# Column sums by transposes, two experts' gathers at a time, and 128-row spreading products in a three-network float32 kernel

## What is computed

```python
# first network, for each of 2 layers: nine modulation vectors of 1024 from c
mod = c_act @ ada_w[l] + ada_b[l]
sh1, sc1, g1, sh2, sc2, g2, sh3, sc3, g3 = jnp.split(mod, N_ADA, axis=-1)
...
x = x + 0.5 * g1[:, None] * swiglu(h, ff_w13[l, 0], ff_w2[l, 0])
# attention of the second and third network: norms over each head's 64 columns
q = rms_norm_2(q.reshape(B, S, FOX_HEADS, HEAD_DIM), fox_g_q[j])
k = rms_norm_2(k.reshape(B, S, FOX_HEADS, HEAD_DIM), fox_g_k[j])
...
# second network: top-2 of 8 experts, each 1024 -> 3584 (gate, up) -> 1024
top_logit, top_idx = lax.top_k(logits, TOP_K)
gates = jax.nn.softmax(top_logit, axis=-1)
ys = swiglu_2(tokens of expert e, w_gate[e], w_up[e], w_down[e]) * gate
out[token] += ys
```

## Time and profile before

| | us |
|---|---|
| median of 3 runs | 3297.51 |
| lowest and highest | 3294.65, 3300.77 |
| the profiled execution, its own time | 3293.94 |
| the profiled execution, span | 3292.1 |
| mean granted TensorE clock | 0.963 of full |

### The profile page before, as it was taken

The page is one execution under the profiler, slowest core; times in us unless marked ns, Lnnn a source line. Parts: engine busy times, 40 slices in busy tenths (PEclk is TensorE's granted clock), DMA queues, the critical chain, the costliest instruction groups (busy, mean ns, idle before and its releaser), DMA issues.

```text
span 3292.1 us, 49368 instructions
## 1 busy us (share of the span) xinstructions
PE 3153.1 (96%) x21206; PEld 2908.7 (88%) x21206; DVE 2261.7 (69%) x2574; ACT 1701.9 (52%) x1910; POOL 84.8 (3%) x163
## 2 busy tenths in 40 slices
PE   6999899999998999999989999999999999989999
PEld 6999899999988998899978888888888888889999
DVE  6686667677555555454575888888888888544575
ACT  4434343443534335443434777777777777444453
POOL 1010001011000000000000000000000000000000
PEclk9999899999988999999987999999999999989999
DMA  7685458678421653245412988989889889423353
GB/s 278 239 305 206 145 193 289 221 278 293 171 71 65 218 203 124 70 144 184 167 39 88 368 338 341 363 338 362 342 337 365 337 341 364 153 103 129 104 192 116
DMA packets 112319, 739.26 MB, mean 225 GB/s; under 512 B 12480, under 2 KB 12480, under 8 KB 32096
## 3 DMA queue, kind: packets, MB, share of 16 engines
q1 hardware_dynamic: 89424, 651.21, 53.1%
q0 software_dynamic: 22672, 84.84, 7.2%
HBM read 734.95 MB, written 1.05 MB: 224 GB/s over the span
## 4 chain that ended last, share of the span: by engine, by line
PE 79%; DVE 5%; ACT 2%; issue 1%; DMA 0%; DVEq 0%; ACTq 0%; POOLq 0%
PE ps L514 60%; PE ps L513 17%; PE ps L523 2%; DVE wlo L2702 2%; DVE AF L2684 1%; ACT whi L1823 1%; DVE att L2693 0%; DVE hl L2675 0%; DVE gf L2687 0%; ACT cv L1811 0%; DVE T L2675 0%; DVE AF L2675 0%; ACT hh L1811 0%; ACT L1811 0%; ACT AF L1811 0%
## 5 line engine op out<-in xcount | busy, mean ns | idle before, releaser
L2702 DVE TENSOR_TENSOR wlo<-ring,whi 128x2048 fp32r<-128x2048 f32 x620 | 1418.7, 2291 | 505.9 <-ACT whi L1823 505.5
L1823 ACT ACTIVATE whi<-ring 128x2048 fp32r<-128x2048 f32 x620 | 1186.0, 1915 | 342.9 <-issue 236.0
L514 PE MATMUL ps<-whi,AR 128*128 128x512 f32 (+1 forms) x2724 | 880.2, 398 | 0.4 <-DVE AF L2675 0.4
L514 PE MATMUL ps<-hh,whi 128*128 128x256 f32 x2464 | 707.5, 287 | 3.9 <-DVE wlo L2702 3.3
L514 PE MATMUL ps<-hl,whi 128*128 128x256 f32 x2464 | 701.3, 285 | 0.0
L514 PE MATMUL ps<-hh,wlo 128*128 128x256 f32 x2464 | 701.3, 285 | 0.0
L514 PEld LDWEIGHTS ps<-whi,AR 128*128 128x128 f32 x2724 | 511.7, 188 | 117.9 <-DVE AF L2675 0.9
L514 PE MATMUL ps<-wlo,AR 128*128 128x512 f32 (+1 forms) x1362 | 536.9, 394 | 0.0
L514 PEld LDWEIGHTS ps<-hh,whi 128*128 128x128 f32 x2464 | 476.1, 193 | 8.6 <-DVE wlo L2702 3.5
L514 PEld LDWEIGHTS ps<-hl,whi 128*128 128x128 f32 x2464 | 476.3, 193 | 0.1
L514 PEld LDWEIGHTS ps<-hh,wlo 128*128 128x128 f32 x2464 | 475.6, 193 | 0.2
(11 more groups left out here) (218 smaller groups left out, 3322.1 us busy)
## 6 DMA issues: line engine op xcount, KB each, us to landing
ring<-in_w SPq DMA_DIRECT2D x620, 1024.0 KB, 4.9
rring<-in_r POOLq DMA_DIRECT2D x151, 512.0 KB, 4.7
AF<-in_mem POOLq DMA_DIRECT2D x2, 1024.0 KB, 6.1
X<-in_x POOLq DMA_DIRECT2D x1, 1024.0 KB, 14.0
AF<-in_cst POOLq DMA_DIRECT2D x1, 1024.0 KB, 5.4
y_out<-X SPq DMA_DIRECT2D x1, 1024.0 KB, 3.8
cst<-in_cst POOLq DMA_DIRECT2D x1, 608.5 KB, 4.4
sm<-in_small POOLq DMA_DIRECT2D x1, 378.0 KB, 4.6
```

The lines of the kernel that those rows point to most:

```text
L514: return self.e.matmul(out, l, r, start=start, stop=stop)
L1823: self.e.activation(N.whi[:, c % HB, :], N.ring[:, c % RING, :], ACT.Copy).then_inc(N.sem["hi"], 1)
L2702: self.e.tensor_tensor(N.wlo[:, c % HB, :], N.ring[:, c % RING, :], N.whi[:, c % HB, :].bitcast(F32), ALU.subtract).then_inc(N.sem["lo"], 1)
```

## The change

**Modulation.** `Pe.ada_sums` transposes the four pieces of `acc` into one bank, and `Dve.ada_sums` sums the 128 columns of each with a `tensor_reduce` out of PSUM, waits for it, and adds the bias.

**Spreading products.** `rT` has 128 rows, zeroed once at the start by two memsets on DVE; the stationary operand is all 128 rows of `ex`, of which only the first 4 are not zero. The sums are the same.

**Experts.** Tokens of two experts are gathered at once, before an even expert: `e_Sel` holds 2 x 128 columns, and each matmul moves 256. The next expert's first up step is pulled ahead of the back products after an even expert, where a gather stood before. `e_zeh`, `e_zel` hold two experts, `e_SelT` and the gate columns four. `head_norm`, which nothing called, goes.

```diff
-        self.rT = [sb(f"rT{i}", [16, S]) for i in range(2)]
+        self.rT = [sb(f"rT{i}", [P, S]) for i in range(2)]
...
-        self.mm(b[:, 0:S], lhs, rT[0:lhs.shape[0], :], True, True).then_inc(
+        self.mm(b[:, 0:S], lhs, rT[:, :], True, True).then_inc(
...
         for i in range(4):
-            t = self.mm(b[:, i:i + 1], self.acc[:, g % 2, i * P:(i + 1) * P], N.ones[:, 0:1], True, True)
+            t = self.tr(b[:, i * P:(i + 1) * P], self.acc[:, g % 2, i * P:(i + 1) * P])
...
-            self.bcast(key, self.N.C("ex")[0:4, k * P:(k + 1) * P], ("bc", k), k == 1)
+            self.bcast(key, self.N.C("ex")[:, k * P:(k + 1) * P], ("bc", k), k == 1)
...
-        for g in range(2):
+        for g in range(4):
             for lo, z in enumerate((N.hh2, N.hl2)):
...
-                for j in range(4):
-                    k = 4 * g + j
+                for j in range(2):
+                    k = 2 * g + j
                     for tb in range(2):
-                        t = self.mm(b[:, j * P:(j + 1) * P], z[:, tb, k * P:(k + 1) * P], Sel[:, tb, :], tb == 0, tb == 1)
+                        t = self.mm(b[:, j * S:(j + 1) * S], z[:, tb, k * P:(k + 1) * P], Sel[:, tb, :], tb == 0, tb == 1)
...
+        for i in range(2):
+            w = slice(i * P, (i + 1) * P)
+            b = self.take((ex + i, "gs"))
+            for tb in range(2):
+                self.mm(b[:, 0:1], SelF[:, tb, w], G[:, tb, ex + i:ex + i + 1], tb == 0, tb == 1)
+            b = self.take((ex + i, "selT"))
+            for tb in range(2):
+                t = self.tr(b[:, tb * P:(tb + 1) * P], SelF[:, tb, w])
...
-        up(0)
-        up(1)
+        if ex % 2 == 0:
+            up(ex, 0)
+        up(ex, 1)
         turn(0)
...
-        if ex < 7:
+        if ex % 2 == 0:
+            up(ex + 1, 0)
+        elif ex < 7:
             self.gather(ex + 1)
...
+        self.e.memset(self.N.rT[0][:, :], 0.0).then_inc(*self.up())
+        self.e.memset(self.N.rT[1][:, :], 0.0).then_inc(*self.up("zeros"))
...
-        self.tt(N.mod[:, l, m], self.ps(("ada", g))[:, 0:4], N.V("ada_b", l)[:, m], ALU.add, ("free", ("ada", g)))
+        cols = N.mod[:, l, m]
+        turned = self.ps(("ada", g)).rearrange("p (a b) -> p a b", a=4)
+        self.e.tensor_reduce(out=cols, in_=turned, axis=AX, op=ALU.add).then_inc(*self.up(("free", ("ada", g))))
+        self.wait_ge("dve", self.here())
+        self.tt(cols, cols, N.V("ada_b", l)[:, m], ALU.add)
...
-        for tb in range(2):
-            self.ts(N.e_Sel[:, tb, :], N.C("iota")[:, 0:P], RK[:, tb, ex:ex + 1], M[:, tb, ex:ex + 1], ALU.is_equal, ALU.mult,
-                    *([(ex, "sel")] if tb else []))
+        for i in range(2):
+            for tb in range(2):
+                at = slice(ex + i, ex + i + 1)
+                self.ts(N.e_Sel[:, tb, i * P:(i + 1) * P], N.C("iota")[:, 0:P], RK[:, tb, at], M[:, tb, at], ALU.is_equal,
+                        ALU.mult, *([(ex, "sel")] if i and tb else []))
...
         for n in range(2):
-            if ex < 7:
-                self.gathered(ex + 1, n)
+            if ex % 2 and ex < 7:
+                self.gathered(ex + 1, 2 * n)
+                self.gathered(ex + 1, 2 * n + 1)
```

More of the change, by code:

```diff
@@ L294, in lay @@
         af.n = ar.n
+        self.e_zeh, self.e_zel = ar.take(2, 8, P), ar.take(2, 8, P)
+        self.e_gh, self.e_gl = ar.take(3, 256), ar.take(3, 256)
+        self.e_SelT = [ar.take(S) for _ in range(4)]
+        self.e_yh, self.e_yl = ar.take(1024), ar.take(1024)
+        assert ar.n <= self.AF.shape[1]
         self.o_w = [af.take(CH), flat2(self.T)]
@@ L1169, in nsa @@
         self.new_x()
-    def head_norm(self, key, x, n):
-        N = self.N
-        self.stat(key, [N.T[:, k, :] for k in range(n)], N.C("half"))
-        self.rows_of(key, 2 * n)
-        for k in range(n):
-            self.bcast(key, N.C("ex")[0:2 * n, k * P:(k + 1) * P], ("bc", k), k == n - 1)
     def pair_stat(self, key):
@@ L2464, in gathered @@
         if ex:
-            self.wait_ge("mm", (ex - 1, "ze_end"))
+            self.wait_ge("mm", (ex - 2, "ze_end"))
         self.wait_ge("mm", (ex, "ze", g, 0))
-        src = self.ps((ex, "ze", g, 0)).rearrange("p (a b) -> p a b", a=4)
-        self.act(self.N.e_zeh[:, 4 * g:4 * g + 4, :], src, ACT.Copy, (ex, "ze", g), ("free", (ex, "ze", g, 0)))
+        src = self.ps((ex, "ze", g, 0)).rearrange("p (a e b) -> p e a b", a=2, e=2)
+        self.act(self.N.e_zeh[:, :, 2 * g:2 * g + 2, :], src, ACT.Copy, (ex, "ze", g), ("free", (ex, "ze", g, 0)))
     def places(self, ex):
-        self.wait_ge("mm", (ex, "selT"))
-        if ex > 1:
-            self.wait_ge("mm", (ex - 2, "y_end"))
-        self.act(self.N.e_SelT[ex % 2], self.ps((ex, "selT"))[:, 0:S], ACT.Copy, (ex, "selT"), ("free", (ex, "selT")))
+        for i in (ex, ex + 1):
+            self.wait_ge("mm", (i, "selT"))
+            if i > 3:
+                self.wait_ge("mm", (i - 4, "y_end"))
+            self.act(self.N.e_SelT[i % 4], self.ps((i, "selT"))[:, 0:S], ACT.Copy, (i, "selT"), ("free", (i, "selT")))
     def gather(self, ex):
-        for g in range(2):
+        for g in range(4):
             self.gathered(ex, g)
@@ L3283, in nsa @@
         self.finish("nsaout", (1, 5))
-    def head_norm(self, key, x, n, gain):
-        self.rinv(key, 2 * n)
-        for k in range(n):
-            self.wait_ge("mm", (key, ("bc", k)))
-            self.stt(x[:, k, :], x[:, k, :], gain, self.ps((key, ("bc", k)))[:, 0:S], ALU.mult, ALU.mult, (key, "h", k),
-                     ("free", (key, ("bc", k))))
     def halved(self, key, x, x2, gain):
@@ L3627, in select @@
         if ex:
-            self.wait_ge("mm", (ex - 1, "sel_end"))
-        for tb in range(2):
-            self.ts(N.e_Sel[:, tb, :], N.C("iota")[:, 0:P], RK[:, tb, ex:ex + 1], M[:, tb, ex:ex + 1], ALU.is_equal, ALU.mult,
-                    *([(ex, "sel")] if tb else []))
+            self.wait_ge("mm", (ex - 2, "sel_end"))
+        for i in range(2):
[3 more added lines that the diff above has]
+                        ALU.mult, *([(ex, "sel")] if i and tb else []))
     def second(self, ex):
@@ L3657, in gathered, with up @@
         if ex:
-            self.wait_ge("mm", (ex - 1, "ze_end"))
+            self.wait_ge("mm", (ex - 2, "ze_end"))
         self.wait_ge("mm", (ex, "ze", g, 1))
-        src = self.ps((ex, "ze", g, 1)).rearrange("p (a b) -> p a b", a=4)
-        self.cp(self.N.e_zel[:, 4 * g:4 * g + 4, :], src, (ex, "ze", g), ("free", (ex, "ze", g, 1)))
+        src = self.ps((ex, "ze", g, 1)).rearrange("p (a e b) -> p e a b", a=2, e=2)
+        self.cp(self.N.e_zel[:, :, 2 * g:2 * g + 2, :], src, (ex, "ze", g), ("free", (ex, "ze", g, 1)))
     def gates(self, ex):
         self.wait_ge("mm", (ex, "selT"))
-        o = 36 + ex % 2
-        if ex > 1:
-            self.wait_ge("act", (ex - 2, "yh", 1))
-            self.wait_ge("dve", (ex - 2, "yl", 1))
+        o = 36 + ex % 4
+        if ex > 3:
+            self.wait_ge("act", (ex - 4, "yh", 1))
+            self.wait_ge("dve", (ex - 4, "yl", 1))
         self.cp(self.N.misc[:, o:o + 1], self.ps((ex, "gs"))[:, 0:1], (ex, "gs"), ("free", (ex, "gs")))
     def gather(self, ex):
-        for g in range(2):
+        for g in range(4):
             self.gathered(ex, g)
         self.gates(ex)
+        self.gates(ex + 1)
     def expert(self, ex):
         N = self.N
-        o = 36 + ex % 2
-        if ex < 7:
+        o = 36 + ex % 4
+        if ex % 2 and ex < 7:
             self.select(ex + 1)
         nf = 14
-        def up(f):
+        def up(ex, f):
             self.chunk()
@@ L3712, in expert @@
                      (ex, "yl", n), ("free", (ex, "y", n)))
-        if ex < 7:
+        if ex % 2 == 0:
+            up(ex + 1, 0)
+        elif ex < 7:
             self.gates(ex + 1)
+            self.gates(ex + 2)
         for k in range(0, 8, 2):
```

59 lines of the change are left out of this document (26 added, 33 removed).

## The result

| | before | changed |
|---|---|---|
| median, us | 3299.14 (4 runs) | 3257.03 (4 runs) |
| lowest and highest | 3294.65, 3302.51 | 3251.73, 3261.34 |
| the profiled execution: own time, span | 3293.94, 3292.1 | 3255.79, 3253.9 |
| its mean granted TensorE clock | 0.963 | 0.966 |

The direction was right, and the work went at the places named; the size was not.

A forecast was written before the change was run, and what follows sets the result against it. PE was taken to bound the feed-forward and expert stages; -13.4 - 13.5 + 1.5 - 1.1 = -26.5 us took the profiled 3293.94 to 3267.4, given as a median of 3269. The 8-in-10 range was 3258 to 3284.

The forecast's parts named there:

- The sum: Whole kernel: experts -13.4, column sums -13.5, opening stage +1.5 and spreading products -1.1 make -26.5 us.
- -13.4 forecast: Expert stage: -9.6 from three later pair gathers, -2.9 at the first pair, -0.9 from back products.
- those 32 cost the same: Opening gather of the experts: 32 matmuls of 256 columns at 1.2 GHz take what 128 columns took, about 0.21 us each.
- The 0.12 per matmul of 256 columns: Pair's gather on PE: 32 matmuls at 0.12 us need 3.84 us, where two single gathers took 7.04.
- Rival A: Experts, four places: splits fall behind and PE waits 3.3 us for a low half, 13 in all; chance 0.07, with B 0.03.
- -13.5 and +1.5 forecast: Column sums: thirty feed-forward blocks save 13.5 us on PE; DVE's reductions before the first norm add 1.5 in the opening.
- DVE's price: Column sums on DVE: a 512-element reduction takes some 0.69 us, 0.78 more per block, covered in feed-forward steps.
- I had 5.9: Opening stage: PE's wait ahead of its first product on the first norm's result grows from 4.39 to about 5.9 us.
- rival C: Feed-forward sums: four transposes drop PE to 1.2 GHz thirty times, 150 us lost, 3419; chance 0.03 with other slow ones.
- -1.1 forecast: Spreading products: 14 pairs, each 0.08 us shorter with 128 rows, save 1.1 us.
- the 0.08 per pair: Spreading products: two of 4 rows take 1.05 us, two of 128 rows 0.97, so 0.08 us saved per pair.
- The next two float32 products: Yardstick for the spreading products: the two behind them, 128 rows deep with as many columns, taking 0.97 us.

The follow-up runs named there:

- -17.3 alone: Only the experts' part of the change, put on the kernel before: ratio 0.9949 (0.9936 to 0.9962), 17.3 us less.
- -15.6 alone: Only the column sums by transposes and a DVE reduction, put on the kernel before: ratio 0.9954 (0.9941 to 0.9967), 15.6 us less.
- -7.4 alone: Only the spreading products with 128 rows, put on the kernel before: ratio 0.9976 (0.9967 to 0.9984), 7.4 us less.

## Why the prediction was right in its places and wrong in its size

**The sum against the time.** Forecast -26.5, measured -41.0 mean against mean (3297.8 to 3256.8), and -38.2 between the two profiled executions. The changed kernel loses 109.0 us to the clock, the one before 127.5; 18.5 x 0.69 = 12.8 us by the fit, and 28.2 us are left for the work, near the sum. By places, without the fit: experts -17.9, column sums -12.9, spreading -3.1, together -33.9; the other 4.3 of the 38.2 are the net of stages with hardly any changed work, 4.2 us gained between chunks 120 and 160 and 2.7 lost between chunk 200 and the gather among them. So the step that failed first is one that was not there: I took the granted clock for a given, put its change at nothing without a reason, and let it only fall, in a rival. It rose. The two countings put its part at 12.8 us (fit) and at about 8 (places: 4.3, and 3.7 at the opening gather). By places the work is then 30.2 us (33.9 less the 3.7 at the opening gather), 3.7 more than the sum, 2.0 of it in the spreading products. Why the clock rose outside the gather stays open.

**Experts, -13.4 forecast; -17.9 between the alignments at the start of the stage (-20.4) and its end (-38.3), -17.3 alone.** By places: four even boundaries 4 x -4.34 = -17.4, forecast -17.3; three odd ones 3 x +0.65 = +2.0, forecast +2.7; the opening -2.5, forecast +1.2. The failed step is "those 32 cost the same" at the opening: it carried the 1.2 GHz level of the trace of before over to a stretch that the change rewrites. The 0.12 per matmul of 256 columns was 0.1175, and the back products behind an even expert 1.91 (forecast 1.92). Rival A did not come: DVE's first low half behind the boundary begins at 1905.49 and ends 2.2 later, 13.7 us after the last down product, which I had counted as 14.6.

**Column sums, -13.5 and +1.5 forecast; -15.6 alone.** From product to product 22 blocks give 0.50 us where 0.49 was in the sum and seven give 0.45 where 0.38 was; the one left, at the end of the first layer, gives nothing, since PE's wait for DVE behind it grew from 0.76 to 1.10 us. That makes 14.2 in all, and 12.9 with the 1.3 of the opening taken off. By alignment the sums alone show -11.8 at the end of the profiled execution, nearly the -12.0 of the sum; most of the rest goes with the clock (0.9626, 3.3 us by the fit). DVE's price was right (0.684 us against 0.69) and hidden in the steps. In the opening PE's wait grew from 4.39 to 5.06; I had 5.9. The +1.3 us by chunk 8 is less sure: chunk 8 came at 99.5 to 102.5 us in six kernels with the old sums there, and at 99.9 to 104.6 in eight with the new. The feared pull of transposes on the clock (rival C) is not there: the layer holds 1.00 with four in each step. (The two transposes of an expert's step, set against this rival at 0.22 us, take 0.13 from their start to the next product's, 1934.38 to 1934.51 in the kernel before.) The Trainium skill says that transposes don't count as PE-busy for the full clock (TensorE: Matmul & The Clock Gate, Part 4, PE-mode transpose); at 0.41 us in 17.70 nothing of that can be seen here.

**Spreading, -1.1 forecast; 3.1 of work, -7.4 alone.** The failed step is the 0.08 per pair. "The next two float32 products" were a poor yardstick: they stood behind the 4-row ones and were lengthened too, and the delay ahead of the pair was not counted. From neighbour to neighbour it is 0.29 us at seven pairs. The Trainium skill (TensorE: Matmul & The Clock Gate, section on LDWEIGHTS) says that a load's time goes by its columns and not by its rows. The trace agrees: 0.185 us with 4 rows, 0.190 with 128. That rows would then bring nothing, as the prediction put it beside its sum, doesn't follow: what they changed is when the loads start.

## What to carry to other kernels

Price an instruction of another shape from the start of its normal predecessor to the start of its successor's successor, not against the row next to it, since a change of shape is paid on both sides. Where PE bounds a stage, read the granted clock beside each place that the change rewrites, and put its rise in the range as well as its fall: here it was between a fifth (by places) and a third (by the fit) of the gain. And an idle PE can cost more than its wait, because what follows may run at half clock, as it did behind two waits of four; work pulled ahead of it is worth that too.

## What the runs showed of the hardware that I had not expected

- A matmul of 128 columns costs nearly what one of 256 costs (0.111 against 0.1175 us) at 2.4 GHz, and at 1.2 GHz as well (0.213 for either).
- PE was busy for 18 of 18 us with matmuls of 128 columns, and the granted clock stayed at 0.53. With 256 columns in the same place it rose 3.7 us into the gather. It is one profiled execution each, but the five other kernels with narrow matmuls and six of the seven others with wide ones fall on the same sides; in the seventh the clock had risen before the gather.
- A wait of 2.34 us in the midst of a stage at 1.00 was followed by the 1.2 GHz level in two places of four; without the wait, the kernel beside it holds 1.00 over the whole stretch.
- Float32 products with 4 or 32 of 128 rows cost the same, and 0.29 us per two more than with 128, where the products around them use all rows and PE doesn't wait; the weight loads last as long, and start later.
- Runs of one kernel differ mostly by their clock: 11 runs of one program went from 3288.58 to 3310.39 us with clocks from 0.965 to 0.957.
